# One core, a two-block model in one launch: masks of two attentions moved to the matrix engine, their units cut in halves

## The reference

```
key_chunk = jnp.arange(S) // CHUNK                    # CHUNK = 64
def block(i):                                         # diff attention, Q_BLOCK = 128
    q_chunk = (start + jnp.arange(Q_BLOCK)) // CHUNK
    mask = key_chunk[None, :] <= q_chunk[:, None]
    s1 = jnp.einsum('bhqd,bhkd->bhqk', q1b, k1) * scale    # width 32
    s2 = jnp.einsum('bhqd,bhkd->bhqk', q2b, k2) * scale    # width 32
    p1 = jax.nn.softmax(jnp.where(mask, s1, NEG_INF), axis=-1)
    p2 = jax.nn.softmax(jnp.where(mask, s2, NEG_INF), axis=-1)
    return jnp.einsum('bhqk,bhkd->bhqd', (p1 - lam * p2), v)
...
def block(i):                                         # forgetting attention
    mask = key_pos[None, :] <= q_pos[:, None]
    s = jnp.einsum('bhqd,bhkd->bhqk', qb, k) * scale + (Fq[..., :, None] - F[..., None, :])
    pr = jax.nn.softmax(jnp.where(mask, s, NEG_INF), axis=-1)
    return jnp.einsum('bhqk,bhkd->bhqd', pr, v)
...
def step(state, inp):                                 # rwkv, one per position
    sa = jnp.einsum('bhvk,bhk->bhv', state, -kk_t)
    state = state * w_t[:, :, None, :] + sa[..., None] * b_t[:, :, None, :] + v_t[..., None] * k_t[:, :, None, :]
    return state, jnp.einsum('bhvk,bhk->bhv', state, r_t)
```

## Time and profile before

| | |
|---|---|
| median of 3 runs | 2393.91 us (2390.57 to 2396.67) |
| profiled execution, its own time | 2392.87 us |
| its span in the trace | 2390.9 us |
| mean granted clock of PE | 0.964 of full speed |
| PE busy, share of the span | 91% |
| DVE busy | 64% |
| ACT busy | 44% |
| forget stage, first layer (239.98 to 309.57 us) | 69.59 us |
| diff stage, first layer (309.57 to 376.43 us) | 66.86 us |

### The profile page before, as it was taken

The page is one execution under the profiler, slowest core; times in us unless marked ns, Lnnn a source line. Parts: engine busy times, 40 slices in busy tenths (PEclk is TensorE's granted clock), DMA queues, the critical chain, the costliest instruction groups (busy, mean ns, idle before and its releaser), DMA issues. The chain is left out here.

```text
span 2390.9 us, 35471 instructions
## 1 busy us (share of the span) xinstructions
PE 2185.5 (91%) x13217; PEld 1741.9 (73%) x13217; DVE 1532.1 (64%) x2178; ACT 1047.0 (44%) x1572; POOL 121.6 (5%) x189
## 2 busy tenths in 40 slices
PE   5998888999999899888899999999997889799994
PEld 4875566788888787566678888888886666688883
DVE  6657466555577565756655557665434665799996
ACT  3444334433341335433433335133234434688884
POOL 0001200000000000110000000000001010111111
PEclk9999999999999999999999999989998999899997
DMA  8650011233335265001123333537505001899995
GB/s 320 217 185 15 2 37 45 80 96 96 96 144 187 90 211 194 24 2 37 35 74 96 96 96 126 199 96 259 186 19 176 1 19 63 340 410 417 417 414 214
DMA packets 95445, 348.53 MB, mean 146 GB/s; under 512 B 12360, under 2 KB 14520, under 8 KB 95056
## 3 DMA queue, kind: packets, MB, share of 16 engines
q1 hardware_dynamic: 88688, 323.67, 38.1%
q0 software_dynamic: 3888, 14.16, 1.5%
q10 hardware_dynamic: 2736, 8.92, 0.9%
HBM read 333.55 MB, written 21.54 MB: 149 GB/s over the span
## 5 line engine op out<-in xcount | busy, mean ns | idle before, releaser
L501 PE MATMUL ps<-a_hi,w_hi 128*128 128x512 f32 x1344 | 536.4, 399 | 28.4 <-DVE h_lo L407 17.6
L503 PE MATMUL ps<-a_hi,w_lo 128*128 128x512 f32 x1344 | 527.6, 393 | 0.0
L502 PE MATMUL ps<-h_lo,w_hi 128*128 128x512 f32 x1280 | 502.3, 392 | 0.0
L465 DVE TENSOR_TENSOR w_lo<-ring,w_hi 128x1024 fp32r<-128x1024 f32 x178 | 218.1, 1226 | 355.6 <-ACT w_hi L460 355.1
L460 ACT ACTIVATE w_hi<-ring 128x1024 fp32r<-128x1024 f32 x178 | 188.1, 1059 | 492.7 <-PE ps L503 487.2
L501 PEld LDWEIGHTS ps<-a_hi,w_hi 128*128 128x128 f32 x1344 | 255.5, 190 | 92.3 <-issue 26.4
L503 PEld LDWEIGHTS ps<-a_hi,w_lo 128*128 128x128 f32 x1344 | 255.3, 190 | 54.4
L502 PEld LDWEIGHTS ps<-h_lo,w_hi 128*128 128x128 f32 x1280 | 243.3, 190 | 51.8 <-issue 2.9
L3385 DVE TENSOR_TENSOR moe_w_lo<-p,moe_w_hi 128x1024 fp32r<-128x1024 f32 x204 | 238.9, 1223 | 17.3 <-ACT moe_w_hi L3482 12.1
L3482 ACT ACTIVATE moe_w_hi<-p 128x1024 fp32r<-128x1024 f32 x204 | 216.1, 1062 | 66.5 <-PE ps L3425 52.3
L2132 PE MATMUL ps<-p_lo,down_hi 128*128 128x512 f32 x352 | 137.0, 389 | 0.0
(11 more groups left out here) (617 smaller groups left out, 3943.4 us busy)
## 6 DMA issues: line engine op xcount, KB each, us to landing
ring<-in_ffn_up SPq DMA_DIRECT2D x88, 512.0 KB, 3.6
ring<-in_w_in SPq DMA_DIRECT2D x72, 512.0 KB, 5.2
p<-in_moe_gate SPq DMA_DIRECT2D x68, 512.0 KB, 6.8
p<-in_moe_up SPq DMA_DIRECT2D x68, 512.0 KB, 7.0
p<-in_moe_down SPq DMA_DIRECT2D x68, 512.0 KB, 7.8
vt<-in_ada SPq DMA_DIRECT2D x64, 512.0 KB, 3.9
p<-in_ada SPq DMA_DIRECT2D x48, 512.0 KB, 5.7
down_raw<-in_ffn_down SPq DMA_DIRECT2D x32, 704.0 KB, 4.9
```

The source lines that it names most:

```text
L465: self.c.nc.vector.tensor_tensor(self.c.w_lo[:, s % 2, :], self.c.slot(s), self.c.w_hi[:, s % 2, :].bitcast(F32), ALU.subtract).then_inc(s ...
L501: nc.tensor.matmul(bank, c.w_hi[:, s % 2, at], hi(kt), start=(kt == self.order[0]), stop=False)
L502: nc.tensor.matmul(bank, c.w_hi[:, s % 2, at], lo(kt), start=False, stop=False)
L503: return nc.tensor.matmul(bank, c.w_lo[:, s % 2, at], hi(kt), start=False, stop=(kt == self.order[-1]))
```

## The change

The three parts stand in the same two stages.

1. **Masks.** The mask is no longer added by DVE. PE writes it to the bank first (a product of the identity with the mask in the forget stage; in the diff stage a product over 32 rows of which one is not zero, `first_rows` with `later_keys`), and the score is accumulated on it. DVE's additions L995 and L1027 are gone.
2. **Scores of the diff stage** use the 32 rows of queries and keys of their head where they lie, at that row position of the matrix engine. POOL no longer makes zero-padded tiles.
3. **Order.** In the diff stage the scores are issued two units ahead and not one, and the maxima of the next unit stand ahead of the mixing of this one; there is a third pair of probability buffers. On PE and ACT each unit is cut in halves, and `halves` makes a plan in which the rwkv steps stand between them: on PE the first half is the score of unit u + 2 and the second the value product of u - 1 and the transposes of u; on ACT the first is the exponential of u + 1 and the second the copy of u. DVE keeps the old plan.

```diff
@@ forget stage, PE
-            eng.matmul(bank, x_q[h % 2][:, i * P:(i + 1) * P], x_k[h % 2][:, 0:nk], start=True, stop=True
-                       ).then_inc(fx["scored"], 1)
+            eng.matmul(bank[:, i * P:], c.const("ident"), c.const("mask_causal"), start=True, stop=False,
+                       skip_group_check=True)
+            eng.matmul(bank, x_q[h % 2][:, i * P:(i + 1) * P], x_k[h % 2][:, 0:nk], start=False, stop=True,
+                       skip_group_check=True).then_inc(fx["scored"], 1)
...
             if u + 2 < NU:
                 score(u + 2)
+            yield
             if u >= 1:
                 sum_values(u - 1)
@@ diff stage, PE
-            if i == 0:
-                eng.wait_ge(fx["spread"], 12 + 2 * (h + 1))
             for m, lane in enumerate(lanes(h)):
                 if u >= 1:
                     eng.wait_ge(df["exped"], 2 * (u - 1) + m + 1)
-                eng.matmul(PS(m)[:, 0:width(u)], d_q[lane][:, i * P:(i + 1) * P], c.p[:, T_B + 2 + h // 2, 0:width(u)],
-                           start=True, stop=True).then_inc(df["scored"], 1)
+                r = slice(32 * lane, 32 * lane + 32)
+                eng.matmul(PS(m)[:, i * P:width(u)], c.const("first_rows")[r, :], c.const("later_keys")[r, :], start=True,
+                           stop=False, skip_group_check=True, tile_position=(32 * lane, 0))
+                eng.matmul(PS(m)[:, 0:width(u)], c.p[r, T_B + h // 2, i * P:(i + 1) * P],
+                           c.p[r, T_B + 2 + h // 2, 0:width(u)], start=False, stop=True, skip_group_check=True,
+                           tile_position=(32 * lane, 0)).then_inc(df["scored"], 1)
...
             if u == 0:
                 score2(0)
-            if u + 1 < NU:
-                score2(u + 1)
+                score2(1)
+            if u + 2 < NU:
+                score2(u + 2)
+            yield
             if u >= 1:
                 sum_values2(u - 1)
@@ diff stage, ACT
             if u == 0:
                 exp2(0)
+            if u + 1 < NU:
+                exp2(u + 1)
+            yield
             eng.wait_ge(df["turned"], u + 1)
             ...
             on(d_prob_t[u % 2][:, 0:width(u)], PS(2)[:, 0:width(u)], ACT.Copy).then_inc(df["copied"], 1)
             if u == NU // 2:
                 take(0)
-            if u + 1 < NU:
-                exp2(u + 1)
-            yield
+            yield
@@ DVE
-            diagonal = PS(u % 2)[:, i * P:(i + 1) * P]
-            eng.tensor_tensor(diagonal, diagonal, c.const("mask_causal"), ALU.add).then_inc(fx["masked"], 1)
-            eng.wait_ge(fx["masked"], u + 1)
...
-                diagonal = PS(m)[:, i * P:(i + 1) * P]
-                eng.tensor_tensor(diagonal, diagonal, c.const("mask_chunk"), ALU.add).then_inc(df["masked"], 1)
-                eng.wait_ge(df["masked"], n + 1)
...
             if u == 0:
                 maximum2(0)
+            if u + 1 < NU:
+                maximum2(u + 1)
...
             eng.scalar_tensor_tensor(p1, p1, r[:, 0:1], p2, ALU.mult, ALU.add).then_inc(df["mixed"], 1)
-            if u + 1 < NU:
-                maximum2(u + 1)
             yield
@@ plan
+def halves(plan):
+
+    order, open_half = [], False
+    for i in plan:
+        if i == 0:
+            order += [0] * (1 + open_half)
+            open_half = True
+        else:
+            order.append(i)
+    return order + [0]
...
+    plan_halves = gating + halves(forget) + halves(diff[:at]) + [3] + halves(diff[at:]) + end
```

More of the change, by code:

```diff
@@ L62 @@
 CONST = [("ident", 128), ("ones", 128), ("bo64", 128), ("bo32", 128), ("perm", 128), ("cos", 512), ("sin", 512),
-         ("mask_causal", 128), ("mask_chunk", 128), ("scan", 512), ("m_ld", 512), ("m_ldT", 512), ("m_loT", 512),
+         ("mask_causal", 128), ("first_rows", 128), ("later_keys", 128), ("scan", 512), ("m_ld", 512), ("m_ldT", 512), ("m_loT", 512),
          ("m_kaT", 512), ("m_r", 512), ("ident4", 512), ("gla_f", 256), ("gla_b", 256), ("eps", 1), ("gn_eps", 1),
@@ L646, in attention_stream @@
     own, other = [slice(0, 64), slice(64, 128)], [slice(64, 128), slice(0, 64)]
-    d_q = [VT(V_D), VT(V_C), at["w"](7), VT(V_C + 1)]
     lanes = lambda h: [2 * h % 4, 2 * h % 4 + 1]
-    d_prob, d_prob_t = [[SC(0), SC(1)], [SC(2), c.p[:, T_D, :]]], [SC(3 + i) for i in range(2)]
+    d_prob = [[SC(0), SC(1)], [SC(2), c.p[:, T_D, :]], [c.p[:, T_C + m, :] for m in range(2)]]
+    d_prob_t = [SC(3 + i) for i in range(2)]
     d_o, d_sq, d_rs = [c.p[:, T_D + 1 + t, :] for t in range(2)], [c.p[:, T_D + 3, :], SC(13)], [c.p[:, T_D, :], c.p[:, T_F, :]]
@@ L677, in spread_head @@
                 chain(eng.tensor_copy(dst[own[side], :], c.p[own[side], tile, :]))
[L679 to L682, removed]
         eng.wait_ge(sg["mixed"], 2)
@@ L845, in pe @@
             for b in range(blocks[u][1] + 1):
-                last = eng.transpose(PS(2)[:, b * P:(b + 1) * P], d_prob[u % 2][0][:, b * P:(b + 1) * P], c.const("ident"))
+                last = eng.transpose(PS(2)[:, b * P:(b + 1) * P], d_prob[u % 3][0][:, b * P:(b + 1) * P], c.const("ident"))
             last.then_inc(df["turned"], 1)
             yield
+        yield
         sum_values2(NU - 1)
@@ L922, in exp2 @@
                 eng.wait_ge(df["maxed"], n + 1)
-                if u >= 2:
-                    eng.wait_ge(df["turned"], u - 1)
-                on(d_prob[u % 2][m][:, 0:width(u)], PS(m)[:, 0:width(u)], ACT.Exp, bias=d_max[:, n:n + 1],
+                if u >= 3:
+                    eng.wait_ge(df["turned"], u - 2)
+                on(d_prob[u % 3][m][:, 0:width(u)], PS(m)[:, 0:width(u)], ACT.Exp, bias=d_max[:, n:n + 1],
                    accum_out=d_sum[:, n:n + 1]).then_inc(df["exped"], 1)
@@ L1021, in maximum2 @@
         def maximum2(u):
-            i = blocks[u][1]
             for m in range(2):
@@ L1040, in dve @@
             eng.wait_ge(df["inv"], 3 * u + 2)
-            p1, p2 = d_prob[u % 2][0][:, 0:width(u)], d_prob[u % 2][1][:, 0:width(u)]
+            p1, p2 = d_prob[u % 3][0][:, 0:width(u)], d_prob[u % 3][1][:, 0:width(u)]
             eng.tensor_scalar(p2, p2, r[:, 1:2], None, ALU.mult).then_inc(df["inv"], 1)
@@ L1821, in mixers @@
     EARLY = 8
-    plan = [1] * b["shift"] + [2] + [0] * a["first"]
-    plan += alternate(a["gating"] + a["prepare"], b["prepare"] + EARLY) + [2]
-    plan += alternate(a["forget"], b["intra"] - EARLY)
-    last = alternate(a["diff"], b["scan"])
-    at = len(last) - 1 - last[::-1].index(0)
-    plan += last[:at] + [3] + last[at:] + [3, 1, 0, 1, 3, 0, 3, 1, 3]
+    gating = [1] * b["shift"] + [2] + [0] * a["first"]
+    gating += alternate(a["gating"] + a["prepare"], b["prepare"] + EARLY) + [2]
+    forget = alternate(a["forget"], b["intra"] - EARLY)
+    diff = alternate(a["diff"], b["scan"])
+    at = len(diff) - 1 - diff[::-1].index(0)
+    end = [3, 1, 0, 1, 3, 0, 3, 1, 3]
+    plan = gating + forget + diff[:at] + [3] + diff[at:] + end
+    plan_halves = gating + halves(forget) + halves(diff[:at]) + [3] + halves(diff[at:]) + end
     opened = open_out_stream(c, att, rw, w_out)
@@ L1840, in _ @@
             c.sweep(pool, [*ahead.loaded, ahead.high, ahead.low])
-            run("pool", streams[:2], [0, 0, 1, 0, 1, 0])
+            run("pool", streams[:2], [0, 0, 1, 0, 1])
         @block.tensor
         def _(pe):
-            run("pe", streams, plan)
+            run("pe", streams, plan_halves)
         @block.scalar
         def _(act):
-            run("act", streams, plan)
+            run("act", streams, plan_halves)
         @block.vector
@@ L3941, in constants @@
     k["mask_causal"] = np.where(n[None, :] <= n[:, None], 0.0, NEG)
-    k["mask_chunk"] = np.where(n[None, :] // 64 <= n[:, None] // 64, 0.0, NEG)
+    lane = n[:, None] % 32 == 0
+    k["first_rows"] = np.where(lane & (n[None, :] < 64), 1.0, 0.0)
+    k["later_keys"] = np.where(lane & (n[None, :] >= 64), NEG, 0.0)
     k["scan"] = np.tile((np.arange(S) % CH != 0).astype(f)[None, :], (P, 1))
```

23 lines of the change are left out of this document (5 added, 18 removed).

## The result

| | before | after |
|---|---|---|
| median | 2393.36 us (2390.57 to 2396.67, 4 runs) | 2438.04 us (2428.55 to 2445.72, 4 runs) |
| ratio | | 1.0184, interval 1.0146 to 1.0223 |
| profiled span | 2390.9 us | 2436.7 us |
| mean granted clock of PE | 0.964 | 0.935 |
| forget stage, each layer | 69.6 us | 57.5 us |

The change made the kernel 1.8% slower, 45 us, where I had forecast 3 us. Two executions ran in a slower state of the chip, one of the kernel before at 2599 us and one of experiment e4 at 4431 us; no ratio or median here takes them in.) The page of the changed kernel: busy time and share of each engine, and PE's clock in 40 slices of the span. They answer to the earlier trace rows.

A forecast was written before the change was run, and what follows sets the result against it. PE, busy 91% of the span, was taken as the bound, gains coming from its waits or work. Forget -9.8 and diff +11.3 us a layer, +3.0 us over two, gave 2397 us; range 2386 to 2409 us.

The forecast's parts named there:

- Forget stage: Forget-stage term: the transposes' wait for DVE's scaling goes, PE gains masks; -9.8 us a layer.
- The half-clock stretches are left as they are: Sum's assumption: two stretches a layer at 1.2 GHz, 3.4 us each, losing 1.7 us each, stay unchanged.
- rival D: Faster, chance 0.13: forget stage without waits keeps the clock (-6.8 us), covered shape changes give -5 us; 2385 us.
- The new wait: Diff stage: scores of u + 2 wait for exponentials of u + 1; +15.6 or +11.3 us a layer.
- The masks alone: Diff stage: masks as PE products, 32 times 0.22 us, 7 us.
- Side by side: Diff stage: a unit's two scores on different rows overlap, so +11.3 us a layer rather than +15.6.
- my slots: Diff stage, scan step to scan step by score width: 3.29 to 4.64 us one after the other, 3.29 to 4.12 overlapped.
- rival C: Slower, chance 0.12: diff-stage idle time drops the clock once more per stage and layer, 4 times 1.7 us; 2404 us.
- the sum: Both stages, both layers: -9.8 + 11.3 = +1.5 us a layer, +3.0 us in all; 2397 us.
- the order's: Diff-stage term for the new order with masks on PE and overlapping scores: +11.3 us a layer.
- if scores of 32 rows took another time for a column: Diff stage: a sign that would show the forecast wrong; given no size.

The follow-up runs named there:

- e4: The changed kernel with diff-stage scores and masks over 64 rows (zero-padded queries) instead of 32; 2437.71 us, ratio 1.0173.
- e3: The changed kernel with diff-stage scores and masks over 128 rows again (zero-padded queries), order and masks on PE kept; 2400.86 us, ratio 1.0026.
- e5: e3 with the diff-stage masks back on DVE, so that stage keeps only the new order; 2400.48 us, ratio 1.0035.
- e6: The kernel before with the forget part of the change, plus diff masks as 128-row products on PE in the old order; 2372.28 us, ratio 0.9909.
- e11: e3 with only the diff-stage masks over 32 rows, scores still over 128; 2449.11 us, ratio 1.023.
- e2: The kernel before with only the diff-stage scores cut to 32 rows, order and masks on DVE as before; 2402.40 us, ratio 1.0044.
- e7: e5 with a repaired order: ACT's exponentials and DVE's maxima of u + 2 in the first half, DVE halved too; 2371.51 us, ratio 0.9901.
- e9: The changed kernel, 32 rows and masks on PE, with the repaired order of e7; 2386.45 us, ratio 0.9984.
- e12: e3 with each diff mask written as two products over all 128 rows, 64 output rows each; 2413.71 us, ratio 1.0089.
- e8: e3 with only the m = 0 scores and masks of the diff stage over 32 rows; 2442.51 us, ratio 1.0202.

## Why the prediction was wrong

- **Forget stage, right, mis-sized.** Forecast -9.8 us, measured -12.1. The wait for DVE went whole. The term that I had left out is the clock: "The half-clock stretches are left as they are", but the stretch of 3.4 us there went with the wait that stood ahead of it (clock 1.00). By the prediction's own price that is 1.7 us of the 2.3; rival D had this term.
- **The new wait, right.** It came where I put it and with its price: with masks on PE and scores one after the other 14.5 us (e3) against 15.6; the order alone was 10.0 us in e5's first layer. The masks alone were 4.2 us (e6) where I had 7.0.
- **Side by side, right in kind.** At full clock the two scores of 512 columns with their masks take 1.84 us from first mask to scan, against 2.36 us in e3 (327.15 to 329.51 us, above). That is the half microsecond that my slots had for this width (4.12 against 4.64 us). It is lost at half clock, where the pair takes 3.00 us.
- **The step that failed** is rival C's price, and with it the sum's sentence on the half-clock stretches. The sum put the clock's cost at nothing, and C let it fall once more in each stage for 3.4 us. It fell for 72 and 78 us of the two diff stages. And I gave waits as the only cause, since both stretches in the earlier trace rows stood behind waits. The waits with full rows leave 0.98 in both layers of e3 and 1.00 and 0.92 in those of e5, some 13 us at half clock at the most. The rows of the products are what I did not weigh: 128 before, 32 after. Over both layers the forget term was off by -4.6 us and the order's by +6.4 us (14.5 for 11.3); the clock's cost by 37 us against e3. These make 39 of the 42 us by which the forecast was off; the rest lies outside the two stages and wasn't followed up.
- The prediction named it as a way to be wrong ("if scores of 32 rows took another time for a column") but gave it no chance and no price. The trace before could not have given the price; it held rwkv's products of 64 rows at clock 0.98 and better, which spoke the other way.

The Trainium skill (TensorE: Matmul & The Clock Gate, Part 2) says that a matmul's throughput goes by the columns that stream through it. It says too that for a weight load the number of rows doesn't matter. Its Part 1, on the clock gate, ties the gate to how busy PE has been. For records at full clock the first two agree with the rows: the weight loads of a score stand as 0.30 us for two over 32 rows (330.72 us in the changed kernel) and over 128 rows (327.37 us in e3), and the two records of a score of 512 columns stand as 1.02 us in the changed kernel (331.39 us above) and as 1.02 us in e3:

```profile
328.56 1.02 PE L827 MATMUL ps<-p,vt 128*128 128x512 f32 x2
```

The busy share of a stage, though, doesn't tell its clock in these runs: with the same columns and much the same share (84% and 80%) the clock was 0.64 with 32 rows and 0.98 with 128.

**What stays open.** What exactly the gate weighs. rwkv's products of 64 rows and 64 columns fill the forget stage and it runs at 1.00, whereas 64-row scores of 128 columns lose the clock (e4); e11 held full clock for its first 25.7 us and lost it only then, with the same mix of work. Whether waits, empty rows or changes of shape count in which part isn't told apart by these runs. That products over a slice of the rows are the cause is shown by four pairs (before and e2, e3 and the changed kernel, e3 and e4, e7 and e9), of which the last differs in the masks too. Such a slice brings two things, the few rows and a row position of its own with a change of shape around it; e12 tested a change of shape alone, but one of the output rows. Why the same kernel falls in one layer and not in the other (e5, e12) is open as well.

## What to carry to other kernels

Before you cut a product to fewer rows to save padding, look what clock its stage has, and test that cut alone: in a stage with waits it can halve the clock for most of the stage, though at full clock a narrow product takes no more time than a wide one. If a score is issued directly behind the transposes and its bank is freed by the engine that also has to copy these, move the consumer (exponential, maximum) ahead too; moving the producer alone makes a wait of it. And read the clock column of each stage beside the busy share, for here the busy share stayed about the same when the clock fell.

## What was not expected of the hardware

- PE's granted clock falls with the rows that the products use: 0.98 to 0.64 in the same stage with the same instructions over 128 or 32 rows, 0.68 over 64.
- It is worse with waits: few rows cost 5.8 us of a stage with few waits (before to e2) and 18.7 us of one with waits (e3 to the changed kernel). With full rows the stages with waits had 13 us at half clock at the most (e5, e12).
- Two narrow products in a unit are enough (e8, e11), 16 to 18 us after the changes of shape are taken off, an estimate.
- A change from a product of 32 rows to one of 128 takes 0.20 us on the weight loads at full clock (0.42 us in e11, 0.22 us in e3).
